# Block 1 of a two-model kernel: the convolution's taps move from the gate tiles to the head tiles, with their sum in PSUM

## The reference, cut to what matters

```
z = h @ w_in + b_in                       # 5192 columns
u_pool, u_conv, q, k, v, qi, ki, wi, gates = split_cols(z, IN_SIZES)
q, k, qi, ki = rope(...)
y_pool = pool_mixer(u_pool, pool_w, pool_scale) @ w_pool_out
# conformer_conv:
a, gate = split(u_conv);  h = a * sigmoid(gate)
h = causal_dwconv(h, dw_w, dw_b)          # 31 taps, 256 channels
y_conv = silu(layer_norm(h, ln_g, ln_b)) @ w_conv_out
# dsa_attention, blocks of 128 queries:
logits = einsum('bqhd,bsd->bqsh', qi, ki)
score = einsum('bqsh,bqh->bqs', relu(logits), wi)   # 8 index heads
idx = top_k(causal(score), 64)            # keys that each query may see
o = softmax attention over the selected keys
g = sigmoid(gates)                        # 3 x 1024 columns
merged = g0*y_pool + g1*y_conv + g2*y_attn;  return merged @ w_o
```

## Time and profile before

| | before |
|---|---|
| median of 3 runs | 2456.99 us (2456.77 to 2460.47) |
| profiled execution, its own time | 2468.51 us |
| its span | 2466.4 us |
| busy, share of the span | PE 90%, PEld 75%, DVE 53%, ACT 42%, POOL 37% |
| mean granted TensorE clock | 0.932 of full speed |
| chain that ended last | PE 65%, DVE 18%, issue 6%, ACT 6%, POOL 5% |
| same, lines | L421 to L423 37%, L1348 3%, L294 on POOL 1% |

### The profile page before, as it was taken

How to read it: one execution, slowest core, us unless ns; L and a number is a source line. 1 busy time by engine, 2 the same in 40 slices (tenths; PEclk the granted TensorE clock), 3 DMA queues, 4 the chain that set the end, 5 groups by cost and what they waited for, 6 DMA issues and landing times.

```text
span 2466.4 us, 39608 instructions
## 1 busy us (share of the span) xinstructions
PE 2223.9 (90%) x14736; PEld 1854.9 (75%) x14736; DVE 1314.5 (53%) x2688; ACT 1033.0 (42%) x1978; POOL 912.5 (37%) x588
## 2 busy tenths in 40 slices
PE   6969899998788998899999898999889899888898
PEld 5868899987788998667766876776778566666677
DVE  4594556547844664356651235556224766723565
ACT  4433466453435654533322244332334445425332
POOL 0444378005453840333422133332313434333443
PEclk8989999989899999899979999999989899888898
DMA  6423556653345655311122321112232111223121
GB/s 220 146 85 107 187 174 193 188 171 113 103 128 172 196 189 188 120 35 44 41 88 68 120 86 56 61 52 73 86 106 92 52 43 35 79 76 120 52 69 52
DMA packets 72848, 262.92 MB, mean 107 GB/s; under 512 B 8032, under 2 KB 10208, under 8 KB 72416
## 3 DMA queue, kind: packets, MB, share of 16 engines
q1 hardware_dynamic: 71392, 256.31, 32.5%
q0 software_dynamic: 1280, 4.20, 0.6%
HBM read 259.43 MB, written 1.05 MB: 106 GB/s over the span
## 4 chain that ended last, share of the span: by engine, by line
PE 65%; DVE 18%; issue 6%; ACT 6%; POOL 5%; DMA 0%; DVEq 0%; ACTq 0%; SPq 0%; POOLq 0%
PE gemm L421 13%; PE gemm L422 12%; PE gemm L423 12%; PE gemm L688 6%; PE score L727 5%; DVE r L1348 3%; PE obank L759 3%; PE tbank L657 3%; DVE d L1294 2%; PE stat L668 1%; PE obank L763 1%; POOL arena L1830 1%; POOL w_lo L294 1%; DVE zt L1256 1%; DVE small L1554 1%
## 5 line engine op out<-in xcount | busy, mean ns | idle before, releaser
L294 POOL TENSOR_TENSOR w_lo<-ring,w_hi 128x1024 fp32r<-128x1024 f32 x252 | 605.6, 2408 | 556.0 <-ACT w_hi L874 554.7
L421 PE MATMUL gemm<-g_hi,w_hi 128*128 128x256 f32 x1344 | 395.2, 294 | 42.3 <-POOL w_lo L294 28.1
L421 PE MATMUL gemm<-h_hi,w_hi 128*128 128x512 f32 (+1 forms) x928 | 388.5, 419 | 12.4 <-DVE h_lo L1635 9.6
L874 ACT ACTIVATE w_hi<-ring 128x1024 fp32r<-128x1024 f32 x344 | 361.7, 1053 | 81.3 <-PE gemm L423 39.9
L422 PE MATMUL gemm<-g_lo,w_hi 128*128 128x256 f32 x1344 | 383.9, 286 | 0.0
L423 PE MATMUL gemm<-g_hi,w_lo 128*128 128x256 f32 x1344 | 383.8, 286 | 0.0
L422 PE MATMUL gemm<-h_lo,w_hi 128*128 128x512 f32 (+1 forms) x928 | 353.1, 381 | 0.0
L423 PE MATMUL gemm<-h_hi,w_lo 128*128 128x512 f32 (+1 forms) x928 | 352.8, 380 | 0.0
L421 PEld LDWEIGHTS gemm<-g_hi,w_hi 128*128 128x128 f32 x1344 | 264.7, 197 | 62.2 <-POOL w_lo L294 36.2
L1189 ACT ACTIVATE pr<-score,small 128x512 f32<-128x512 f32 (+1 forms) x192 | 128.0, 669 | 392.8 <-DVE small L1556 390.5
L421 PEld LDWEIGHTS gemm<-h_hi,w_hi 128*128 128x128 f32 x928 | 180.5, 195 | 148.4 <-issue 108.2
(11 more groups left out here) (278 smaller groups left out, 3885.4 us busy)
## 6 DMA issues: line engine op xcount, KB each, us to landing
ring<-wall SPq DMA_DIRECT2D x478, 512.0 KB, 3.7
r<-nbias POOLq DMA_DIRECT2D x16, 256.0 KB, 3.0
cst<-consts SPq DMA_DIRECT2D x1, 2340.5 KB, 10.3
r<-x_t SPq DMA_DIRECT2D x1, 1024.0 KB, 4.7
x<-ctx_t SPq DMA_DIRECT2D x1, 1024.0 KB, 15.5
y_t<-x SPq DMA_DIRECT2D x4, 256.0 KB, 2.3
d<-pos SPq DMA_DIRECT2D x1, 128.0 KB, 10.2
```

The lines of the kernel that those rows point to most:

```text
L294: eng.tensor_tensor(w_lo[:, q % SPLITS, :, :], ring[:, t % RING, :, :], w_hi[:, q % SPLITS, :, :].bitcast(F), ALU.subtract)\
L421: pe.matmul(out, w[0][:, k, :], x[0], start=start, stop=False)
L874: act.activation(w_hi[:, q % SPLITS, :, :], ring[:, t % RING, :, :], ACT.Copy).then_inc(S["hi_ready"], 1)
```

## The change

It reorders the head tiles: tiles 0 to 3 are now the convolution input (0: value half 0, 1: its gate, 2 and 3: half 1), 4 is `ki`, 5 to 8 the index queries, 9 is `v`, 10 and 11 pooling, 12 to 16 as they were. The 62 taps run on DVE in head tiles 2 to 16, 4 or 5 per tile, each waiting for the one before, and the running sum lies in PSUM (`tb`, called tbank in the trace); only the last tap of a half writes to SBUF. Some splits of head tiles go from DVE to POOL and two of the gate tiles from POOL to DVE. ACT rectifies the scores in place in PSUM, and DVE reads them there. The mean is taken at gate 1, the variance at gate 3, the normalization is finished at gate 4, the convolution's activation runs at gate 12 instead of 21, and the selection at gate 8. Lines that are only moved or deleted are cut here:

```
-    after_norm(2 * l, "heads", l, "DDDDD" + "R" + "D" * 11)
-    put("gates", l, "P" * NG)
+    after_norm(2 * l, "heads", l, "DD" + "DPDPDPD" + "R" + "PDPDPDP")
+    put("gates", l, "PPDPPDPP" + "P" * (NG - 8))
...
+    state["split"] = t
...
-    eng.wait_ge(S["s_relu"], 8 * l + i + 1)
+    eng.wait_ge(S["relu_used"], 8 * l + i + 1)
...
-    for _ in range(2):
+    for _ in range(1 + 5):
...
-    for _ in range(4 + 2 + 5):
+    for _ in range(2 + 5):
...
-    if i == 9:
+    if i == 1:
-    if i == 10:
+    if i == 3:
...
+    for j in range(2):
+        b = op(0, early) if j == 0 else op()
+        seq(act.activation(zt[:, j, 0:T], b[:, 0:T], ACT.Identity, bias=half[:, l, 2 * j:2 * j + 1], scale=0.5))
+        act.sem_inc(S["bank_read"], 1)
+        if j == 1:
+            ada_columns_all(FILL[2 * l])
+        b = op(0, early + 1) if j == 0 else op()
+        seq(act.activation(zt[:, j, T:2 * T], b[:, 0:T], ACT.Tanh, bias=half[:, l, 2 * j + 1:2 * j + 2], scale=0.5))
+        act.sem_inc(S["bank_read"], 1)
+        act.sem_inc(S["conv_ab"], 1)
...
-    if 8 * l + i >= 2:
-        act.wait_ge(S["relu_used"], 8 * l + i - 1)
-    if i == 0:
-        act.wait_ge(S["roped"], 10 * l + 10)
-    act.activation(relu[:, i % 2, :], sbk[i % 2][:, 0:384], ACT.Relu).then_inc(S["s_relu"], 1)
+    act.activation(sbk[i % 2][:, 0:384], sbk[i % 2][:, 0:384], ACT.Relu).then_inc(S["s_relu"], 1)
...
-    if i == 9:
+    if i == 1:
-    if i == 10:
+    if i == 3:
-        act.activation(zh[:, 0, 0:T], rstd[:, 0:T], ACT.Square).then_inc(S["crstd"], 1)
-    if i == 21:
+        act.activation(pr[:, 1, 0:T], rstd[:, 0:T], ACT.Square).then_inc(S["crstd"], 1)
+    if i == 12:
...
+    def conv_input(j):
+    def conv_taps():
+        for j in range(2):
+            acc = tb[:, j * T:(j + 1) * T]
+            dve.wait_ge(S["conv_in"], 2 * l + j + 1)
+            for k in range(TAPS):
+                w = cc(f"taps{l}", j * TAPS + k)
+                win = cpad[:, j, k:k + T]
+                if k == 0:
+                    seq(dve.tensor_scalar(acc, win, w, cc(f"dw_b{l}", j), ALU.mult, ALU.add))
+                elif k < TAPS - 1:
+                    seq(dve.scalar_tensor_tensor(acc, win, w, acc, ALU.mult, ALU.add))
+                else:
+                    ins = dve.scalar_tensor_tensor(cacc[:, j, :], win, w, acc, ALU.mult, ALU.add)
+                    if j == 0:
+                        seq(ins)
+                    else:
+                        ins.then_inc(S["conv_done"], 1)
+                yield
+    conv = conv_taps()
+    def taps(k):
+        for _ in range(k):
+            next(conv, None)
+    split_to(first + 2)
+    conv_input(0)
+    for t in range(2, 17):
+        split_to(first + t + AHEAD)
+        taps(4 if 4 <= t < 9 or t > 11 else 5)
+        if t == 3:
+            conv_input(1)
+        elif t == 4:
+            rope(10 * l, T, cos1, ki1)
+        elif t < 9 and t > 4:
+            rope(10 * l + t - 4, T, cos1, qi1[:, t - 5, :])
+        elif t == 12:
+            rope(10 * l + 5, T, cos1, k1)
+        elif t > 12:
+            rope(10 * l + t - 7, T, cos1, q1[:, t - 13, :])
...
-                ins = dve.tensor_scalar(score[:, a:z], relu[:, i % 2, a:z], w, None, ALU.mult)
+                ins = dve.tensor_scalar(score[:, a:z], sbk[i % 2][:, a:z], w, None, ALU.mult)
-                ins = dve.scalar_tensor_tensor(score[:, a:z], relu[:, i % 2, a:z], w, score[:, a:z], ALU.mult, ALU.add)
+                ins = dve.scalar_tensor_tensor(score[:, a:z], sbk[i % 2][:, a:z], w, score[:, a:z], ALU.mult, ALU.add)
...
-    if i == 9:
+    if i == 1:
+    if i == 4:
+        x = st[:, T:2 * T]
+        dve.wait_ge(S["crstd"], l + 1)
+        dve.wait_ge(S["conv_centred"], l + 1)
+        seq(dve.tensor_scalar(x, x, LN_EPS, None, ALU.add))
+        seq(dve.scalar_tensor_tensor(x, pr[:, 1, 0:T], -0.5, x, ALU.mult, ALU.mult))
+        seq(dve.scalar_tensor_tensor(x, x, 1.5, rstd[:, 0:T], ALU.add, ALU.mult))
+        for j in range(2):
+            ins = dve.scalar_tensor_tensor(cacc[:, j, :], cacc[:, j, :], cc(f"cln_g{l}", j), x, ALU.mult, ALU.mult)
+            if j == 0:
+                seq(ins)
+        ins.then_inc(S["conv_n"], 1)
+    if i == 8:
...
+    split_to(AT["heads", l] + 3 + AHEAD)
+        split_to(AT["heads", l] + 4 + j + AHEAD)
...
-    pool.wait_ge(slot_used[t % RING], t // RING + 1)
+    pool.wait_ge(slot_used[n["split"] % RING], n["split"] // RING + 1)
...
+    for j in range(2):
+        for o in (0, 256):
+            tiles.append(w_tile(w[:, OFF_CONV + o + j * P:OFF_CONV + o + (j + 1) * P]))
+        if j == 0:
+            fill(4 * FILL[2 * l])
-        if c == 0:
-            fill(4 * FILL[2 * l])
-    for j in range(2):
-        for o in (0, 256):
-            tiles.append(w_tile(w[:, OFF_CONV + o + j * P:OFF_CONV + o + (j + 1) * P]))
```

51 lines of the change are left out of this document (3 added, 48 removed).

## The result

| | before | after |
|---|---|---|
| median of 4 runs each, us | 2458.7 | 2423.6 |
| spread of the runs, us | 2456.8 to 2462.3 | 2415.1 to 2431.6 |
| profiled execution's own time, us | 2468.5 | 2420.4 |
| layer 0: first index score, us | 99.5 | 113.7 |
| layer 0: from there to the first attention score | 85.6 | 52.1 |

The ratio is 0.984, with a 95% interval from 0.9818 to 0.9863: faster, by 1.4 to 1.8%. A second comparison of the same two kernels (run r1_after_again) gave 0.9821 (0.9798 to 0.9844). The forecast was 2409 with 2392 to 2438 around it.

What follows compares the result with a forecast made beforehand. Taps standing still while POOL works left PE idle in gates 0 to 9 of two layers. Per layer 24.6 us less 0.6 for PE's clock is 24.0, two layers 48, so the median goes from 2457.0 to 2409; range 2392 to 2438.

Steps and rivals of the forecast that it cites:

- The bound: Layers 0 and 1: only gates 0 to 9 are not bound by PE; about 2 x 23 us of idle PE to win.
- Price of a tap: Heads, VectorE: 429 ns with one tensor in PSUM, 0.47 us a tap, 62 taps 29.1 us, no standing still.
- Rival 3: PSUM does not free the taps: each costs 829 ns, 22 us more per layer, 2453 us; chance 3%.
- Hold-ups by POOL: Heads: POOL's splits between turns delay the sine product, 2.3 us each; one and a half taken, 3.5 us per layer.
- rival 4: Heads: a 7.0 us ring of waits through VectorE, POOL and PE at every turned tile; slower, 2465 us; chance 6%.
- The last turn: Heads of layer 0: VectorE's last turn done at 110.6 us; gate 0 starts at 105.5 us, after POOL's split.
- The gates: Gates 0 to 14: PE sets the pace, 55.0 us in all, with 2 us of stall for ACT's two table loads.
- The selection: VectorE, gates: 19.1 us from near 138 to near 157 us, hidden, 3 us ahead of gate 15.
- Attention gates: Stage after gate 14: bound by PE, keeps its 41.9 us, and what follows is untouched.
- rival 1: Heads and gates: clock stays at 0.84, about 8 us more per layer, 2425; or late selection, 2419; chance 14%.
- rival 2: Heads: hold-ups at most turns without closing a ring, 10 to 20 us lost per layer, 2429 to 2449; chance 9%.

Runs made afterwards that it cites:

- The longer selection: The changed kernel with 26 more maximum searches behind the selection of each layer, results unused; 2434.8 us in one run.

## Why the prediction was right, and where it was not

**The sign and the range were right**: the gates were bound by taps that stood still, and PSUM frees them. The time itself was 14.6 us over the 2409 forecast, and steps 2 and 5 say why. The steps, in the prediction's order:

1. *The bound.* Right in the gates. A slip in the cut: the first window of the earlier trace rows held gate 0, so "what PE does in the heads takes 50 us" should have been 46, and "nearly as today" compared gate 0 with gate 1. Rightly counted, my own numbers had the heads 6.0 us longer (99.5 to 105.5) and the gates 30.6 shorter (85.6 to 55.0). The 24.6 us that come out are the same, since the time of gate 0 came from VectorE's sum; but "the taps are hidden" was wrong already on paper.
2. *Price of a tap*: this failed in size. I took 0.43 us and 0.47 from one to the next. Measured, ahead of the first convolution input, nine taps in one row:

```profile
55.38 4.69 DVE L1321 SCALAR_TENSOR_TENSOR tbank<-r,cst,tbank 128x256 f32<-128x256 f32 x9
```

0.52 each, 62 x 0.05 = 3.1 us more per layer. The row I chose, L1267, has a constant as scalar, and the taps have a column; the run with a constant shows that this is the whole difference in the length of a tap (428 ns against L1267's 429). I matched where the tensors lie and overlooked the scalar, which L1348's own 485 ns in the earlier trace rows had in it.
3. *The rule of the Trainium skill* ("VectorE: DVE Perf Modes", section on the TRN2 errata), by which an operation with a PSUM source takes 62 cycles more than one with an SBUF source. Not seen: 490 ns in PSUM, 485 in SBUF, in one and the same place. The taps did come out 60 ns over my price, near the 65 of that rule, and only the run with a constant shows that it is not the rule's doing. My own evidence against the rule, 429 ns with PSUM beside 472 with SBUF, compared a constant scalar with a column and showed nothing.
4. *Taps are not held*: right, a maximum of 490 ns after. Rival 3 is out.
5. *Hold-ups by POOL*: this failed in size and in kind. I took 3.5 us, and as price a sine product late behind a split. That wait stayed 0.62 us in all ten turns, so rival 4's ring did not form either. What stood still were VectorE's own operations with two SBUF inputs, the turns' sum and cosine product and one split: 2.17, 2.12 and 0.44 us over their own time (sums at 65.24, 79.97 and 85.90), 0.45, 0.44 and 2.19 (cosine products at 108.52, 112.79 and 115.33), 0.43 (split at 100.70), 8.2 us together. I had the mechanism in hand for the taps and did not ask it of the turns. The Trainium skill says it ("SBUF — State Buffer", section "SBUF: two separate sides"): a VectorE operation with two SBUF inputs and a GpSimd operation that reads SBUF exclude each other for the whole instruction, and the one that starts first wins. The 0.07 us between 65.17 and 65.24 agree, and that it holds for every such operation is what my step lacked.
6. *The last turn* at 110.6 was 118.98: 3.1 of taps, 4.7 of hold-ups, 0.6 of the rest. Gate 0 at 105.5 was 113.7, 8.2 late. The turn of tile 14, behind which POOL makes gate 0's split, ended at 110.4 and not at 103.3: 2.9 of taps, 3.6 of hold-ups (5.6 by then where I had 2.0), 0.6 of the rest. A window sum of 0.85 us stands between that turn and the split, which I had left out, and makes up most of the last 1.1. That the hold-ups of step 5 also sum to 8.2 is chance: the last of them, 2.19, comes behind the start of gate 0. The heads took 59.3 us where I had written 51 to 53. The hold-ups are the term that was most mis-sized.
7. *The gates*: 55.0 forecast, 52.1 measured, 2.9 better. The two table loads cost PE nothing. ACT, then VectorE's next sum:

```profile
130.38 1.28 ACT L998 ACT_TABLE_LOAD   x1
...
132.17 1.28 ACT L999 ACT_TABLE_LOAD   x1
...
134.74 0.87 DVE L1360 SCALAR_TENSOR_TENSOR scratch<-score,arena,scratch 128x128 f32<-128x128 f32 x2 [5.02 <-ACT score L974]
```

VectorE waits 5.02 us there, but the tiles split ahead carry PE over it, so the 2 us were not due. The three small products take 0.87 each, not 1.
8. *The selection*: hidden, as said. It ran from 144.5 to 159.8 us, without the hold-ups of the earlier trace rows, and VectorE then stood idle 7.1 us; "3 us of slack" was cautious: it ended 6 us ahead of the first attention score. The longer selection showed that this is slack.
9. *Attention gates*: 43.5 against 44.0, as forecast.

In sum, layer 0: 24.6 forecast, less the 8.2 by which gate 0 was late, plus 2.9, is 19.3, the difference between 185.1 and 165.8. That leaves 39 us for both layers where I had 48, and the medians came to 35 us in one comparison and 44 in the other. The time came to lie near that of rival 1 (2425), whose falling clock is there too: 0.86 in the heads. That is chance: VectorE waits for neither PE nor ACT in the heads, so the lower clock did not set its pace, and the gates ran at full clock. Whoever had bet on rival 1 would have had the number for the wrong reason. A part of rival 2 is what happened: hold-ups of 8.2 us where that rival began at 10.

## What to carry to other kernels

Here a VectorE operation that reads two SBUF tensors stood still until GpSimd's current operation ended, for up to 2.2 us, and none of the 116 taps and 20 turn sums with one tensor in PSUM did; that one edit for the taps gave two thirds or more of a change that also rewrote the order. When work is moved into a stage, count the operations already there that now meet the other engine, and look at each engine's weight splits queued behind them: freeing the taps moved the hold-ups to the score sums where the taps stayed in the gates (7.8 us), to the turns where they went to the heads (8.2 us with one split), and then to a split. When a price is borrowed from another line, match every operand, the scalar too.
